# Attention of a hybrid two-layer model: both kinds of head in one run, the third group of transposes moved behind the next score products and evicted by DVE

## What is computed

```python
def attend(q, k, v, scale):
    s = jnp.einsum('bhgqd,bhkd->bhgqk', q, k).astype(jnp.float32) * scale
    p = jax.nn.softmax(s, axis=-1).astype(v.dtype)
    return jnp.einsum('bhgqk,bhkd->bhgqd', p, v)
...
    oa = blocked_attend(qa_x, cat(ka_x, ka_c), cat(va_x, va_c), A_SCALE)
    ob = blocked_attend(qb_x, cat(kb_x, kb_c), cat(vb_x, vb_c), B_SCALE)
...
    oa_c = attend(qa_c, ka_c, va_c, A_SCALE)
    ob_c = attend(qb_c, kb_c, vb_c, B_SCALE)
```

## Time and profile before

| | us |
|---|---|
| median of 3 runs | 4232.28 |
| lowest and highest run | 4231.64, 4232.49 |
| the profiled execution | 4226.73 |
| span of its trace | 4224.9 |

### The profile page before, as it was taken

The page is one execution under the profiler, slowest core; times in us unless marked ns, Lnnn a source line. Parts: engine busy times, 40 slices in busy tenths (PEclk is TensorE's granted clock), DMA queues, the critical chain, the costliest instruction groups (busy, mean ns, idle before and its releaser), DMA issues. The chain is left out here.

```text
span 4224.9 us, 44523 instructions
## 1 busy us (share of the span) xinstructions
PE 3667.2 (87%) x17492; PEld 2713.8 (64%) x17492; DVE 1786.6 (42%) x2458; ACT 1258.7 (30%) x2138; POOL 134.6 (3%) x108
## 2 busy tenths in 40 slices
PE   6987788788895999999995999756898759999997
PEld 3663466566673888888883877432344538888885
DVE  2222556555407333333336432775255244333334
ACT  3322467666524111111114222220100232221122
POOL 0000000000001000000001000310000010000001
PEclk7998899999997999999998999875999979999998
DMA  7623310110003111111103210001320121111112
GB/s 292 252 93 101 92 26 14 50 35 17 25 17 124 40 36 38 40 37 37 40 25 119 90 50 22 1 34 60 123 84 25 60 94 51 46 49 50 50 45 94
DMA packets 98569, 272.31 MB, mean 64 GB/s; under 512 B 18205, under 2 KB 33053, under 8 KB 94276
## 3 DMA queue, kind: packets, MB, share of 16 engines
q1 hardware_dynamic: 98436, 270.51, 18.9%
HBM read 220.41 MB, written 50.07 MB: 64 GB/s over the span
## 5 line engine op out<-in xcount | busy, mean ns | idle before, releaser
L569 PE MATMUL psum<-h_high,w_high 128*128 128x512 f32 (+1 forms) x1280 | 472.7, 369 | 51.3 <-DVE w_low L648 51.3
L569 PE MATMUL psum<-h_low,w_high 128*128 128x512 f32 (+1 forms) x1280 | 472.3, 369 | 0.0
L569 PE MATMUL psum<-h_high,w_low 128*128 128x512 f32 (+1 forms) x1280 | 471.8, 369 | 0.0
L582 PE MATMUL psum<-hid_low,w_high 128*128 128x512 f32 (+1 forms) x1280 | 471.5, 368 | 0.0
L582 PE MATMUL psum<-hid_high,w_high 128*128 128x512 f32 (+1 forms) x1280 | 471.3, 368 | 0.0
L582 PE MATMUL psum<-hid_high,w_low 128*128 128x512 f32 (+1 forms) x1280 | 470.8, 368 | 0.0
L513 PE MATMUL psum<-h_high,w_high 128*128 128x512 f32 (+1 forms) x944 | 367.8, 390 | 37.3 <-DVE w_low L506 24.4
L645 DVE TENSOR_TENSOR out<-out,psum 128x512 f32<-128x512 f32 x320 | 202.7, 634 | 463.3 <-PE psum L582 463.3
L513 PE MATMUL psum<-h_high,w_low 128*128 128x512 f32 (+1 forms) x944 | 349.3, 370 | 0.0
L513 PE MATMUL psum<-h_low,w_high 128*128 128x512 f32 (+1 forms) x944 | 348.8, 370 | 0.0
L595 ACT ACTIVATE w_high<-w_raw 128x1024 fp32r<-128x1024 f32 x126 | 132.7, 1053 | 663.2 <-PE psum L582 662.8
(11 more groups left out here) (359 smaller groups left out, 5449.3 us busy)
## 6 DMA issues: line engine op xcount, KB each, us to landing
w_raw<-in_ff_w_dram SPq DMA_DIRECT2D x128, 512.0 KB
ada_ring<-in_ada_w_dram SPq DMA_DIRECT2D x24, 2048.0 KB, 8.7
scratch_x<-x SPq DMA_DIRECT2D x6, 2048.0 KB, 7.2
x<-scratch_x SPq DMA_DIRECT2D x6, 2048.0 KB
x<-in_x_dram SPq DMA_DIRECT2D x4, 2048.0 KB, 11.8
w_raw<-in_w_out_dram SPq DMA_DIRECT2D x16, 512.0 KB
scratch_spectra<-spectrum_out SPq DMA_DIRECT2D x32, 256.0 KB, 2.0
filter_ring<-scratch_spectra SPq DMA_DIRECT2D x16, 512.0 KB, 4.9
```

Source lines behind the costliest of these rows:

```text
L569: mm = pe.matmul(g.ps[:, u % BANKS, 0:n], x[:, k, :], y[:, k, a:a + n], start=(k == 0 and i == 0), stop=(k == KT - 1 and i == 2))
L582: mm = pe.matmul(g.ps[:, BANKS + u % BANKS, 0:n], x[:, k * 2 + half, :], y[:, k, a:a + n], start=(k == 0 and i == 0), stop=(k == HT - 1 an ...
```

## The change

The loop over kinds goes: one set of buffers and semaphores and one block serve all eight pairs, x runs from 0 to 159, and the buffer of the low part of the queries, which kind 0 doesn't use, exists throughout. The last pair of kind 0 now prepares the four items of the first pair of kind 1.

The third group of step x-3 is issued in iteration x, behind the scores of x. The mix moves from iterations with x mod 4 = 2 to those with x mod 4 = 3, behind that third group. The third group is copied out by DVE (`tensor_copy`, at the head of its iteration, ahead of the maximum of x), the other two groups and the mix by ACT as before. The single counter `emptied` is replaced by `turned_out` (ACT's evictions), `last_out` (DVE's) and `mixed_out`; `bank_free` waits on whichever belongs to the use two before. The second group of step x-2 then follows the third group of step x-3 in the same bank.

```diff
-    for kind in range(2):
-        rows = slice(0, (P, B_DK)[kind])
...
-        with stage(nc, names) as (mem, sems):
...
+    for x in range(N + LAG + 1 + PER):
+        if has_turn(x - LAG - 1, 2):
+            use["turn", x - LAG - 1, 2] = len(use)
+            dve_turns[x - LAG - 1] = len(dve_turns)
+        if mix_due(x) is not None:
+            use["mix", mix_due(x)] = len(use)
+        for j in range(2):
+            if has_turn(x - LAG, j):
+                use["turn", x - LAG, j] = len(use)
+                act_turns[x - LAG, j] = len(act_turns)
...
+    with stage(nc, names) as (mem, sems):
...
+                def bank_free(r):
+                    if r < 2:
+                        return
+                    key = user[r - 2]
+                    if key[0] == "mix":
+                        pe.wait_ge(mixed_out, key[1] + 1)
+                    elif key[2] == 2:
+                        pe.wait_ge(last_out, dve_turns[key[1]] + 1)
+                    else:
+                        pe.wait_ge(turned_out, act_turns[key[1], key[2]] + 1)
...
+                for x in range(N + LAG + 1 + PER):
+                    if x < N:
+                        scores_of(x)
+                    if has_turn(x - LAG - 1, 2):
+                        turn(x - LAG - 1, 2)
+                    if mix_due(x) is not None:
+                        mix(mix_due(x))
+                    for j in range(2):
+                        if has_turn(x - LAG, j):
+                            turn(x - LAG, j)
...
+                for x in range(N + LAG + 1):
+                    if has_turn(x - LAG - 1, 2):
+                        dst, src = turned_to(x - LAG - 1, 2)
+                        dve.wait_ge(filled, use["turn", x - LAG - 1, 2] + 1)
+                        dve.tensor_copy(dst, src).then_inc(last_out, 1)
+                    if x < N:
+                        dve.wait_ge(scores, x + 1)
...
+                    for j in range(2):
+                        if has_turn(x - LAG, j):
+                            dst, src = turned_to(x - LAG, j)
+                            act.wait_ge(filled, use["turn", x - LAG, j] + 1)
+                            act.activation(dst, src, ACT.Copy).then_inc(turned_out, 1)
```

More of the change, by code:

```diff
@@ L1039, in attention @@
 def attention(nc, g, sc, out):
[L1047 to L1053, removed]
-    N = len(ALL)
+    PAIRS, KINDS = 4, 2
+    LAG = 2
+    QB = 2 * P
+    B, PER = TOK // QB, 4
+    S = B * PER
+    ALL = [(pair, i) for pair in range(KINDS * PAIRS) for i in range(S)]
+    N = len(ALL)
+    ITEMS = (((0, 0), (0, 1), (1, 0)), ((0, 0), (0, 1), (1, 0), (1, 1)))
@@ L1056, in keys_of, with kind_of, step @@
+    COPIES = (2, 1)
+    ROWS = (slice(0, P), slice(0, B_DK))
+    jobs = [(pair, n) for pair in range(KINDS * PAIRS) for n in range(len(ITEMS[pair // PAIRS]))]
+    job_of = {job: m for m, job in enumerate(jobs)}
+    def kind_of(pair):
+        return pair // PAIRS
+    def step(x):
+        pair, i = ALL[x]
+        return pair, i // PER, i // 2 % 2, i % 2
     def keys_of(b):
         return (0, KTILES) if b < LAT // QB else (LAT // P, KTILES)
-    def block_of(x):
-        return steps[ALL[x][1]][0]
@@ L1062, in width, with raw_total @@
     def width(x):
-        lo, hi = keys_of(block_of(x))
+        lo, hi = keys_of(step(x)[1])
         return (hi - lo) * P
     def turns(x):
-        lo, hi = keys_of(block_of(x))
+        lo, hi = keys_of(step(x)[1])
         return [(i, min(i + 4, hi)) for i in range(lo, hi, 4)]
[L1072 to L1078, removed]
+    def raw_total(m):
+        return 16 * sum(COPIES[kind_of(jobs[i][0])] for i in range(m % 2, m + 1, 2))
@@ new lines, in v_total, with mix_due, has_turn @@
+    def v_total(pair):
+        return 16 * sum(COPIES[kind_of(i)] for i in range(pair % 2, pair + 1, 2))
+    def mix_due(x):
+        y, off = divmod(x - LAG - 1 - PER, PER)
+        return y if off == 0 and 0 <= y < N // PER else None
+    def has_turn(x, j):
+        return 0 <= x < N and j < len(turns(x))
+    use, act_turns, dve_turns = {}, {}, {}
+    for x in range(N + LAG + 1 + PER):
[8 more added lines that the diff above has]
+                act_turns[x - LAG, j] = len(act_turns)
@@ L1080, in last_turn @@
+    user = {r: key for key, r in use.items()}
     def last_turn(x):
         return use["turn", x, len(turns(x)) - 1]
[L1083 to L1244 removed]
@@ new lines, in _ @@
+                        act.activation(out[:, pair, b * QB:(b + 1) * QB], g.ps[:, 6 + r % 2, 0:QB], ACT.Copy).then_inc(mixed_out, 1)
+                    for j in range(2):
[3 more added lines that the diff above has]
+                            act.activation(dst, src, ACT.Copy).then_inc(turned_out, 1)
+                    if x < N:
+                        act.wait_ge(maxed, x + 1)
+                        if x >= 3:
+                            act.wait_ge(filled, last_turn(x - 3) + 1)
+                        if x >= 4:
+                            act.wait_ge(inverse, x - 3)
+                        act.activation(p[:, x % 3, 0:width(x)], scores_flat(x), ACT.Exp, bias=neg_max[:, x % 4:x % 4 + 1],
+                                       accum_out=total[:, x % 4:x % 4 + 1]).then_inc(exped, 1)
+                        if split_at(x):
+                            round_item(*split_at(x))
```

197 lines of the change are left out of this document (139 added, 58 removed).

## The result

The changed kernel takes **4239.24 us** (median of 7 runs, 4235.68 to 4246.89), beside 4231.64 for seven runs of the kernel before (4228.30 to 4232.49). The ratio is 1.0027, 95% interval 1.0017 to 1.0036. So the changed kernel is 0.3% slower, a small loss but clear of no change. Forecast were 4239.7 and a range of 4221 to 4250. The point was met; two groups of its terms were off in ways that nearly cancelled.

A forecast was written before the change was run, and what follows sets the result against it. No engine is full; plain steps are bound by ACT in kind 0, by PE in kind 1. Terms -6.5 - 10.6 - 5 - 24.5 + 34.8 + 19.2 = +7.4 us on 4232.28 gave 4239.7 us; range 4221 to 4250.

The forecast's parts named there:

- Plain steps, mixes, ends: Attention steps without items, mixes behind long blocks, seams between pairs: -6.5 (kind 1 only), -10.6 and -5 us.
- The seam of the kinds: Between the two kinds, a gap of 27.42 us becomes an ordinary seam of 2.95: -24.5 us.
- The items after: Visible items in the changed kernel cost 3.1 us each in kind 0, 2.7 in kind 1; net of before +34.8.
- The clock: PE's clock halves at about 18 of 21 item stalls, against six falls before, 1.6 us each: +19.2 us net.
- Items and clock of the kernel before: Pairs with items, before: items cost 4.2 us a pair in kind 0, 4.7 in kind 1, a clock fall 1.6.
- The clock holds: Rival: at the item stalls falls come no more often than before, +19.2 goes, result 4220.5 us; chance 0.16.
- Falls at each stall and stays down: Rival: PE's clock falls at all 21 item stalls, half of them double, +38 us, result 4258.5; chance 0.16.
- The wait goes for good: Rival: PE's 69.3 us wait for the third group's bank vanishes, sum -59 us, result 4173; chance 0.04.
- The copy runs at twice the rate: Rival: DVE's copy out of PSUM reaches the second speed tier, -0.13 us a step; given no chance.

The follow-up runs named there:

- e2: The changed kernel with the two kinds kept apart again, so only the third group's move remains: 4246.63 us, ratio 1.0030 to the kernel before.
- e3: The changed kernel with nine additional score products at each item, issued where PE would stand idle, results overwritten: 4214.76 us, ratio 0.9955 to the kernel before.
- e1: Both kinds merged in one run, with the order of the kernel before and all groups evicted by ACT: 4212.97 us, ratio 0.9956 to the kernel before.
- e8: The changed kernel with items behind i = 2, 6, 10, 14 and DVE's split one iteration later: 4150.51 us, ratio 0.9805 to the kernel before.
- e9: e1 with items behind i = 1, 5, 9, 13 and DVE's split one iteration later: 4169.81 us, ratio 0.9855 to the kernel before.
- e6: The changed kernel with items behind i = 2, 6, 10, 14, each followed by a step with a mix: 4166.07 us, ratio 0.9844 to the kernel before.
- e7: The changed kernel with DVE's split one iteration later, items left where they are: 4159.91 us, ratio 0.9828 to the kernel before.
- e4: The changed kernel with the third group in its new place but copied by ACT instead of DVE: 4204.16 us, ratio 0.9922 to the kernel before.

## Why the prediction was right

**Plain steps, mixes, ends: right in kind, a quarter too small.** Steps are 2.72 us in kind 0 (forecast: no gain from 2.73) and 3.13 in kind 1 (3.12), but there the first behind each mix stays at 3.31 to 3.33, so only two of three gain. The copy takes 0.422 us (0.42). What a pair without items gains is read from the table and the seams: the last pair of kind 1 from 74.19 to 70.52, its seam from 3.53 to 2.98; in kind 0, 66.25 to 63.83 (the fourth pair of e2, 91.15 less its seam of 27.32) from first to last exponential, and the seam from 2.95 to 2.41. So 3.0 us for each of three pairs of kind 0, 2.4 for the fourth, 4.2 for each of three of kind 1 and 3.7 for the last: 27.6 us, where the three terms gave 6.5 + 10.6 + 5 = 22.1. The plain steps gave less than their term: 24 of 36 gain 0.17, some 4 us beside 6.5. The mixes gave more: 0.44 us in kind 0 and 0.54 in kind 1 where 0.33 was forecast, 11.8 us for the three of each pair that can be read by themselves beside 7.9. The rest, some 12 us, lies in the short steps, the fourth mix and the first steps of a pair, beside 7.6. The cause that was forecast for mixes and ends, one eviction less ahead of the exponential, is worth 0.33 us each; no run tells what the rest is.

**The seam of the kinds: right.** 27.42 to 3.00 us is -24.4; forecast -24.5.

**The items after: right.** e3 gives them without the clock. Pairs of kind 0 take 75.90 and would take 63.83 + 2.41 without items, 9.66 us for three (forecast 9.3); those of kind 1 take 83.49 - 1.96 = 81.53 against 70.52 + 2.98, so 8.03 (8.1). The fourth pair comes to 78.05 - 1.96 - 63.83 - 2.98 = 9.28 (9.3). In all 62.3 us, forecast 61.5.

**The clock: its direction right, the count too small and the price too high.** I said 18 falls and 19 lengths at 1.6 us, 30.4. The trace has 19 falls, but 26 lengths. Their cost is the difference of the pairs of after and of e3, less e3's own 1.96 where it applies: 2.8 (against e3's 75.90), 3.9, 2.4, 3.7, 6.8, 7.1, 7.2, together 33.9 us, or 1.3 a length. In kind 0 that is 12.8 us for 11 lengths, 1.2; in kind 1, where PE is the bound, 21.1 for 15, 1.4. Six of the seven doubled stretches lie in kind 1. At the forecast's own price 26 lengths would have been 41.6 us and the forecast 4250.9, outside its range. The point was met by luck here: the price was wrong the other way.

**Items and clock of the kernel before: slightly overrated.** Their sum is 35.3 us (the pairs of before less 69.20 or 77.72 each); the forecast's parts came to 26.7 + 7 x 1.6 = 37.9. In kind 0 e1 tells them apart, since its third pair has the same order and no fall: 73.52 less 69.20 is 4.3 us for three items (forecast 4.2), and the 75.03 of the third pair of before is 1.5 more for its one fall (1.6); e1's second pair, with a fall, is 1.2 more. In kind 1 no run has a pair in this order without a fall.

Together: -27.6 - 24.4 + 62.3 + 33.9 - 35.3 = +8.9, beside the 8.8 of the table and the +7.4 forecast. The terms that failed are two sizes. Items and clock came to 62.3 + 33.9 - 35.3 = +60.9 where the forecast had 34.8 + 19.2 = +54.0. Half of the difference is the clock's 33.9 us after, beside 30.4. Plain steps, mixes and ends came to -27.6 instead of -22.1. The errors are 7 and 5.5 us with opposite signs, so the point was met more closely than its parts were known. Either alone would have left the result inside the range.

**The rivals.** *The clock holds* is out: 19 of 21 stalls brought a fall, and e3, in which it does hold, is 25 us faster. *Falls at each stall and stays down* was half right: about a third were doubled rather than half, and its 31 lengths at 1.6 were 26 at 1.3. By the count the result lies nearer to this rival than to the forecast's 19, by the cost nearer to the forecast. The Trainium skill, "TensorE: Matmul & The Clock Gate", section "HAM oscillation — how this bites in real kernels", tells of a loop with waits of about 3 to 5 us between bursts of products, in which the full clock is lost every time. The stalls here are 2.9 us, a little shorter, and the trace agrees at 19 of 21. *The wait goes for good* is out as the program stands. Even in e8, where nothing stands ahead of the copy for long, 16.9 us of it are left, and the gain over e9 is 25 us and not 69. In kind 0 the reason is the one that the forecast gave against it, steps of 2.73 us bound by ACT and of 2.72 with the copy on DVE. *The copy runs at twice the rate* is out: it took 0.422 us.

What I did not see is how much hangs on this one chain: the items' steps (e6) or the split's place (e7), an edit of a line or two, take 72 and 78 us out of attention, eight and nine times what the change put in. The forecast had the chain and its price, but not that a line could take it out.

## What to carry to other kernels

An instruction moved to a less busy engine inherits whatever that engine is waiting for. Here the copy cost 0.42 us and stood behind a split that waited for ACT; read what stands in front of the new place, not the busy share.

When work on one engine is moved by a step, look for what it used to hide: the mix hid the items, and the line that says which steps carry an item has to move along.

If a change has two parts, measure each alone: here one gained 0.4% and the other lost 0.3%, and rejecting both together would have thrown away a gain, and with the items moved along a second.

## What was not expected of the hardware

PE idle in one piece of 2.9 us was followed by half the clock in 19 of 21 places, and inside the pairs the low stretches came only in two lengths, those shown 3.2 and 6.6 us (3.35 and 6.70 in the earlier trace rows). Nine additional products at each item, 2.33 us together, whose results nobody reads, kept the clock at 1.00 from 482 us on, to the end of attention, and made the kernel 25 us faster.

In e4 the same idle time, cut in two by transposes and scores, mostly left the clock up, whereas in the kernel before idle pieces of 1.56 and 2.03 us were followed by a fall. What the difference is between the two was not tried.
